# Third block of a three-block transformer kernel: output gate placed among the dense products, scratch moved out of the weight buffers, memory outcomes one direction behind, attention outputs divided instead of probabilities

## The reference, cut to what matters

```
h    = modulate(rms_norm(x), shift, scale)
proj = h @ w_in            # 1024 x 2832, columns: q 512, k 128, v 128, qk_m 1024, v_m 512, o_m 512, gates 16
y_attn = attention(rope(rms(q)), rope(rms(k)), v)          # 8 heads of 64, 2 key heads, not causal, softmax
qk     = silu(depthwise_conv5(qk_m))                       # queries and keys of the memory, 4 heads of 128
h_fw, h_bw = matrix-memory recurrence forwards and backwards, with input and forget gates, per head
y_mem  = rms(h_fw + h_bw) * norm_g * sigmoid(o_m)
x = x + g1 * (concat(y_attn, y_mem) @ w_out)
x = x + g2 * ((silu(h2 @ w_gate) * (h2 @ w_up)) @ w_down);  out = rms_norm(x)
```

## Time and profile before

| what | us |
|---|---|
| median of three runs (1934.21 to 1938.34) | 1935.97 |
| the profiled execution: its time | 1942.17 |
| its span, first to last instruction | 1940.4 |
| PE busy in the span | 1869.4 (96%) |
| DVE busy | 1168.7 (60%) |
| ACT busy | 737.5 (38%) |
| POOL busy | 127.6 (7%) |

### The profile page before, as it was taken

One profiled execution on the slowest core, in us unless ns is written; L12 is line 12 of the kernel. 1 busy time (PEld: TensorE's weight loads), 2 busy tenths in 40 slices (PEclk: granted clock), 3 DMA queues, 4 the chain that ended last, 5 costly groups with the idle time before them and its releaser, 6 DMA issues.

```text
span 1940.4 us, 22966 instructions
## 1 busy us (share of the span) xinstructions
PE 1869.4 (96%) x9180; PEld 1506.2 (78%) x9180; DVE 1168.7 (60%) x2110; ACT 737.5 (38%) x1154; POOL 127.6 (7%) x113
## 2 busy tenths in 40 slices
PE   9999999999999999999999999789898899999997
PEld 7775888878878788788888888677556698888885
DVE  4987686545566785578445446767775554333437
ACT  4458343322233434544222232535554352222221
POOL 0331000000000251000000000000230000000000
PEclk9999999999999999999999999899999899999998
DMA  6221425344441221224433432131001413323221
GB/s 204 66 71 34 158 90 193 131 144 138 152 153 45 87 66 44 87 87 152 130 108 118 139 113 89 27 106 44 1 1 66 141 33 102 105 87 109 87 87 44
DMA packets 118282, 186.17 MB, mean 96 GB/s; under 512 B 7472, under 2 KB 72176, under 8 KB 115104
## 3 DMA queue, kind: packets, MB, share of 16 engines
q1 hardware_dynamic: 116784, 179.90, 28.1%
q0 software_dynamic: 1392, 4.82, 0.8%
HBM read 182.57 MB, written 2.13 MB: 95 GB/s over the span
## 4 chain that ended last, share of the span: by engine, by line
PE 76%; DVE 16%; ACT 5%; issue 3%; POOL 0%; DMA 0%; DVEq 0%; ACTq 0%
PE bank L602 10%; PE bank L603 10%; PE bank L604 10%; PE bank L794 7%; PE bank L795 7%; PE bank L793 7%; DVE wl L1896 2%; PE bank L576 2%; PE bank L578 2%; PE bank L577 2%; PE bank L855 2%; PE bank L839 2%; DVE gb L2272 2%; DVE m L2270 1%; PE bank L827 1%
## 5 line engine op out<-in xcount | busy, mean ns | idle before, releaser
L1896 DVE TENSOR_TENSOR wl<-raw,wh 128x2048 fp32r<-128x2048 f32 (+1 forms) x137 | 307.6, 2251 | 195.2 <-ACT wh L1267 195.0
L1267 ACT ACTIVATE wh<-raw 128x2048 fp32r<-128x2048 f32 (+1 forms) x142 | 265.2, 1883 | 238.8 <-PE bank L795 90.5
L602 PE MATMUL bank<-xh,wh 128*128 128x512 f32 (+2 forms) x880 | 347.4, 395 | 2.2 <-DVE wl L1896 2.2
L603 PE MATMUL bank<-xh,wl 128*128 128x512 f32 (+2 forms) x880 | 346.7, 394 | 0.0
L604 PE MATMUL bank<-xl,wh 128*128 128x512 f32 (+2 forms) x880 | 346.7, 394 | 0.0
L795 PE MATMUL bank<-wh,ul 128*128 128x512 f32 x592 | 230.4, 389 | 0.0
L794 PE MATMUL bank<-wl,uh 128*128 128x512 f32 x592 | 230.4, 389 | 0.0
L793 PE MATMUL bank<-wh,uh 128*128 128x512 f32 x592 | 230.3, 389 | 0.0
L602 PEld LDWEIGHTS bank<-xh,wh 128*128 128x128 f32 (+2 forms) x880 | 164.9, 187 | 42.8 <-DVE wl L1896 3.1
L604 PEld LDWEIGHTS bank<-xl,wh 128*128 128x128 f32 (+2 forms) x880 | 165.0, 188 | 38.7
L603 PEld LDWEIGHTS bank<-xh,wl 128*128 128x128 f32 (+2 forms) x880 | 165.0, 187 | 38.1
(11 more groups left out here) (367 smaller groups left out, 3082.2 us busy)
## 6 DMA issues: line engine op xcount, KB each, us to landing
raw<-in_mlp_w_up SPq DMA_DIRECT2D x32, 1024.0 KB, 5.7
raw<-in_mlp_w_down SPq DMA_DIRECT2D x32, 1024.0 KB, 5.1
raw<-in_w_ada SPq DMA_DIRECT2D x24, 1024.0 KB, 5.2
raw<-in_b_w_in SPq DMA_DIRECT2D x12, 1024.0 KB, 5.2
raw<-in_w_in SPq DMA_DIRECT2D x11, 1024.0 KB, 5.1
raw<-in_w_gate SPq DMA_DIRECT2D x11, 1024.0 KB, 5.3
raw<-in_w_up SPq DMA_DIRECT2D x11, 1024.0 KB, 5.3
raw<-in_w_down SPq DMA_DIRECT2D x10, 1024.0 KB, 5.0
```

What stands on the lines that cost most here:

```text
L602: pe.matmul(o, H[:, k, c], xh[:, k, :], start=k == 0, stop=False)
L603: pe.matmul(o, L[:, k, c], xh[:, k, :], start=False, stop=False)
L1267: act.activation(slots[slot_of[i]][0][:, 0:n], raw[:, i % NRAW, 0:n], ACT.Copy).then_inc(*s_high.up(i))
L1896: dve.tensor_tensor(L[:, 0:n], raw[:, i % NRAW, 0:n], H[:, 0:n].bitcast(F), ALU.subtract).then_inc(*s_low.up(i))
```

## The change: what it does

Dense products: the 16 gate columns are appended to the keys' piece (two pieces of 4 x 272 columns instead of one of 8 x 256, `gates` and `ggT` go). The output gate's product `og` becomes an ordinary dense product between the second and third `conv`, its sigmoid is taken as its tiles are read. The order is `k2`, two `conv`, `og`, two `conv`, `v2`. All small jobs are numbered by step, from 0 to 31, and end with `v2`; the first two steps of `heads` are made at steps 28 and 30.

Middle: only `heads` and `memory` remain, in `side_by_side`: one step each for eight rounds, then one of `heads` and two of `memory`. The scratch moves to the halves of x (`xf`, which lies under `xh` and `xl`), to `pl` and to the halves of u (`rz`); `STm` and `Dd` get two buffers, `Db` three. The banks are shared out: 0 to 3 for scores, turned probabilities and inverses, 4 for the attention's output, 5 for `M`, 6 and 7 for `S` and `hm`. The outcomes of pair m are made during the scores of pair m + 1. `D` is one DVE instruction for four cells, and POOL masks it (`affine_select`). The probabilities are no longer divided: the inverses of the sums are turned, sent through DRAM to all partitions (`spread`), and POOL multiplies the outputs.

Tail: pieces of `w_out` are fetched and split during the middle. `first_column(0)` comes before `G` and `ymT`, `first_column(1)` behind them.

```diff
@@ weight_plan
-    plan_tok(w2, 512, 256)
-    slots(1, 0)
-    plan(w2, 0, 8, 2816, 16)
-    plan_tok(w2, 1792, 512)
-    for n in range(4):
+    for r0 in (0, 512):
+        plan(w2, r0, 4, 512, 256)
+        parts, nk, n = chunks[-1]
+        gates = w2[r0:r0 + 512, 2816:2832].rearrange("(k p) n -> p k n", p=P)
+        chunks[-1] = (parts + [(gates, n, 16)], nk, n + 16)
+    slots(0, 1)
+    for n in range(2):
         plan(w2, 0, 8, 768 + n * 256, 256)
     plan_tok(w2, 2304, 512)
...
+    plan_tok(w2, 1792, 512)
@@ buffers and banks
+def side_by_side(heads, mem, over):
+
+    live, n = [heads, mem], 0
+    while live:
+        for job in (heads, mem) if n < 8 else (heads, mem, mem):
+            if job in live and next(job, over) is over:
+                live.remove(job)
+        n += 1
...
+        B_UNITS, B_OUT, B_MAX, B_MEM, ANY = range(4), (4,), (5,), (6, 7), range(8)
...
+        DIVIDED = {"A": 7, "B": 4}
...
-        STm = rawf[:, 2048:4096].rearrange("p (b s) -> p b s", b=T)
+        PTs = [xf[:, 2048 * i:2048 * i + 2048].rearrange("p (b s) -> p b s", b=T) for i in range(2)]
+        STm = [xf[:, 4096 + 2048 * i:6144 + 2048 * i].rearrange("p (b s) -> p b s", b=T) for i in range(2)]
+        PB2 = [pl[:, 4 + i] for i in range(4)]
@@ tensor_program
+            def small_jobs():
+                for step in range(32):
+                    if step == 10:
+                        turn("qT2", tm, 4, s_step.at("rope q"))
+                    if step in (13, 14):
+                        gates(step - 13)
+                    if step == 20:
+                        turn("kT2", kd2, 2, s_step.at("rope k"))
+                    if step in (22, 26):
+                        gate_columns((step - 22) // 4)
+                    if step in (28, 30):
+                        next(heads)
+                    yield
...
                 start(0)
+                for m in range(len(MEM) + 1):
+                    for t in range(T):
                         yield
+                        if m < len(MEM):
+                            score(m, t)
+                        if m and t % 2 == 0:
+                            outcome(m - 1, t // 2)
+                        if m + 1 < len(MEM) and t == 2:
+                            start(m + 1)
+
+            side_by_side(heads, memory(), jobs)
...
+            first_column(0, cur.take(skip))
             for n, gc in enumerate((GC1, GC2)):
...
+            first_column(1, cur.take(skip, 2))
             cross("o3", UH, UL, 4, u_ready, 4, False, "x5", [("gate", 0, 0), ("upg", 0, 0)], xo, lambda t: s_act.at(("xo", t)))
@@ scalar_program
+                        if k < len(CELLS) and CELLS[k] in OFF:
+                            decay(*CELLS[k])
+                        if m + 1 < len(MEM) and t == T - 1:
+                            own(m + 1)
+                        if 0 < m <= len(MEM) and t % 2 == 0:
+                            size(m - 1, t // 2)
@@ vector_program, memory
+                        if m + 1 < len(MEM) and t == 3:
+                            own(m + 1)
+                        if m < len(MEM):
+                            weigh(m, t)
+                        if m and t % 2:
+                            divide(m - 1, t // 2)
+                        if m == 3 and t == 0:
+                            cur.reach(low, 2)
@@ POOL
-            attend("B", PB2, 8, False)
+                    w.wait_ge(*s_step.at(("D", m)))
+                    pool.affine_select(Dd[m % 2], Dd[m % 2], [[0, T], [1 - 2 * d, P]], ALU.is_ge, -BIG, 0, 2 * d - 1).then_inc(*s_pool.up(("D", m)))
@@ SP
-            w.wait_ge(*s_mm.at("middle"))
-            for i in range(core2, len(chunks)):
-                w.wait_ge(*low_of(i - NRAW))
-                fetch(i)
+                if i == mixed[2] + 3:
+                    for j in range(4):
+                        spread("B", j)
```

More of the change, by code:

```diff
@@ L114, in restart, with take @@
         self.order, self.user, self.before = list(range(8)), [None] * 8, {}
-    def take(self, name, hold=False):
-        b = self.order.pop(0)
+    def take(self, name, hold=False, among=range(8)):
+        b = next(b for b in self.order if b in among)
+        self.order.remove(b)
         if not hold:
@@ L1108, in small_jobs @@
-                yield from idle(2)
-                turn("kT2", kd2, 2, s_step.at("rope k"))
-                turned.append("k")
-                b = banks.take("ggT")
-                w.wait_ge(*banks.free("ggT", s_act.sem))
-                w.wait_ge(*s_act.at(("gates", 0)))
-                for t in range(T):
-                    step = pe.transpose(bank[b][:, t * 16:(t + 1) * 16], ggf[:, t * P:(t + 1) * P], ident[0:16, 0:16])
-                step.then_inc(*s_turn.up("ggT"))
-                yield from idle(3)
@@ L1118, in small_jobs @@
-                yield from gates(0)
-                yield from gates(1)
-            jobs.append(small_jobs())
-            gemm_tok("k2", 256, "x4", 1)
-            gemm_T("gates", "x4", 2)
-            gemm_tok("v2", 512, "x4", 2)
-            Wo = []
-            for n in range(4):
-                gemm_T(("conv", n), "x4", 2,
-                       (lambda: Wo.extend([cur.take(skip), cur.take(skip, 0)])) if n == 3 else None)
-            while len(turned) < 2:
-                tick(jobs)
@@ L1162, in start, with score @@
                     pe.matmul(bank[b][:, :], sel, Mr[d], start=True, stop=True).then_inc(*s_mm.up(("M", m)))
+                def score(m, t):
+                    hh = MEM[m][0]
+                    c0, c1_ = keys(m, t)
+                    b = banks.take(("S", m, t), False, B_MEM)
+                    w.wait_ge(*banks.free(("S", m, t), s_act.sem))
+                    w.wait_ge(*s_act.at(("conv", 7)))
+                    pe.matmul(bank[b][:, 0:c1_ - c0], mqk[:, 4 + hh, t * P:(t + 1) * P], mqk[:, hh, c0:c1_],
+                              start=True, stop=True).then_inc(*s_mm.up(("S", m, t)))
@@ new lines, in outcome @@
+                def outcome(m, tt):
+                    hh, d = MEM[m]
+                    b = banks.take(("hm", m, tt), False, B_MEM)
+                    w.wait_ge(*banks.free(("hm", m, tt), s_act.sem))
+                    w.wait_ge(*s_step.at(("ST", m, T - 1)))
+                    w.wait_ge(*s_act.at(("v2", T - 1)))
+                    w.wait_ge(*s_step.at("vx1"))
+                    for t in (2 * tt, 2 * tt + 1):
+                        src = list(range(0, t + 1) if d == 0 else range(t, T))
+                        o = (t % 2) * 256
+                        for q in src:
+                            step = pe.matmul(bank[b][:, o:o + 130], STm[m % 2][:, q, t * P:(t + 1) * P], vx[:, q, hh, :],
+                                             start=q == src[0], stop=q == src[-1])
+                    step.then_inc(*s_mm.up(("hm", m, tt)))
@@ L2600, in memory, with own @@
+            gemm_tok("k2", None, 1)
+            for n in range(2):
+                gemm_T(("conv", n), lambda j: evict_c(n, j), 1)
+            gemm_tok("og", None, 1)
+            for n in range(2, 4):
+                gemm_T(("conv", n), lambda j: evict_c(n, j), 1)
+            gemm_tok("v2", None, 1)
+            drain(jobs)
             def memory():
-                for job in rest:
-                    yield from job
-                def start(m):
+                def own(m):
                     hh, d = MEM[m]
-                    mk = CBT if d == 0 else CB
+                    M = bank[banks.of["M", m]][:, :].rearrange("p (t q) -> p t q", t=T)
@@ L2672, in vector_program @@
+            side_by_side(heads, memory(), jobs)
+            cur.take(low)
             w.wait_ge(*s_act.at(("hsq", T - 1, 3)))
```

789 lines of the change are left out of this document (355 added, 434 removed).

## The result

The changed kernel takes 1954.95 us (median of 4 runs, 1952.07 to 1958.85) where the kernel before takes 1936.11 on the same chip: a ratio of 1.0098, interval 1.0077 to 1.0119. It is 1% slower; 1912 us and "faster" were forecast. The profiled execution took 1955.38 us, its span 1953.6.

What follows compares the result with a forecast made beforehand. PE's list was taken as the bound, lengthened by waits of several engines. 111.8 + 116.2 + 5.8 = 233.8 against 257.5 us, 23.7 less: 1936.0 - 23.7 = 1912 us; own range 1902 to 1922, 8 in 10 for 1896 to 1928.

Steps and rivals of the forecast that it cites:

- dense products, less the earlier start: Dense products: 106.8 us of work, less 2.0 for the earlier start, plus 4 of waits and 3 of lower clock: 111.8.
- middle: Attention and memory stage: 94.6 us of PE work, 18.6 of holes and 3 for the clock behind them: 116.2.
- tail: Up to the first `w_out` product: `G` 3.7, turns 1.8, entry 0.3, both old waits gone: 5.8 us.
- the holes are hidden in 16 of 22 rounds: Middle: attention work in front of each two cells covers the bank waits; only rounds 16 to 21 bare, 11 us.
- A clock below 0.9 in the middle: Middle: listed among the observations that would show the prediction wrong; no time was attached to this sign.
- the clock falls: Rival, middle: lower clock in most later rounds, some 30 us lost, 1945 to 1960 us in all; chance 7%.
- the clock's term: Middle: 3 us for PE running at a lower clock behind the 18.6 us of holes.
- The 3.6 us that I put for `M`: Middle: next pair's `M` waits until ACT has read a backward pair's last `Db`, twice 1.8 us: 3.6.
- under PE's work: Middle: DVE's split of the `w_out` piece is hidden by PE's work; no time was put for it.
- a sum of differences is not touched by that: Baseline: the profiled execution's 6.2 us above the median 1936.0 was taken not to affect the predicted 23.7 us gain.
- The waits for the gates: Dense products: second direction's gates asked for some 3 us too early; 4 us put for this and the first `conv` piece.
- The mask: Middle: POOL's mask of `D` put at 1.8 us, between 0.7 and 3.7, making the next pair's hole 3 us.

Runs made afterwards that it cites:

- the kernel with the other phase: Changed kernel with one more single step at the start (n < 9 for n < 8), so late rounds hold cells 0, 1 or 2, 3: 1927.96 us.
- the run with `og` ahead: Kernel before, with only the output gate's product moved out of the middle, as a dense stretch ahead of it: 1949.42 us, ratio 1.0068.
- the fastest kernel: Changed kernel with division before weighing, memory pairs in rounds 1 to 14, gate columns and gates' turns later, `w_out` split behind `ym`: 1896.73 us.
- a kernel that differs by an earlier edit only: Changed kernel with division before weighing, memory pairs in rounds 1 to 14, second gate columns a step later: 1909.09 us; without the last edit 1918.51.

## Why the prediction was wrong

The stages, reckoned as there, from the first product of the keys to the first with `w_out`. The changed kernel starts this stretch 5.1 us earlier (1254.05 for 1259.19). The prediction put 2.0 for that.

| term | predicted | measured |
|---|---|---|
| dense products, less the earlier start | 111.8 | 119.6 - 5.1 = 114.5 |
| middle | 116.2 | 147.9 |
| tail | 5.8 | 5.9 |
| sum | 233.8 | 268.3 |

**The step that failed** is "the holes are hidden in 16 of 22 rounds". I had worked out the waits themselves correctly: S2 waits for the division of O0, S0 of the next pair for that of O1, 1.7 to 3 us each. But I took a late round to hold cells (0, 1) or (2, 3), so that an attention step stood in front of each cell that waits. It holds (1, 2) and (3, 0), since the generator's first `next` makes no cell. The order that is printed ahead of the prediction shows it: the cells come two by two without a row of the attention between them, and it is the second that needs the bank. So the mechanism was right and its place was wrong. In place of 18.6 us of waits there were 33.5, and the kernel with the other phase has 18.7.

**The clock** was the second part. A clock below 0.9 in the middle stood among the signs of being wrong, and it came. I put 3 us for it. With 94.6 + 3 = 97.6 us of busy time expected and 114.5 measured, it took nearly 17 more. My rival "the clock falls" named 1945 to 1960 us, "when the middle takes 140 us"; it took 148, and this rival comes nearest to what happened. I gave it 7%. Its number was better than its way there: it put some 30 us for the clock, of which 17 to 20 came, and most of the rest was waits that stood in the wrong rounds. I argued against it from the clock of the old middle; but there `og` filled the turns, and the run with `og` ahead (0.93 for 0.96, in one execution each) suggests that this filler was part of the reason. The Trainium skill (TensorE: Matmul & The Clock Gate, A second HAM failure mode: psum-queue depth-cycling) says that frequent short idle times between groups of matmuls, from cycling through PSUM banks, make the clock go back and forth; the trace agrees, with waits of 1.5 to 3.8 us for two banks and a clock of 0.85.

**Even in the right phase the forecast was too low.** The kernel that I had in mind exists: it is the one with the phase alone, 1928.0, the end of my range. Its middle takes 118.5 us from the first `M`, and 120.6 from the end of the dense products (1373.21 to 1493.82), 4.4 above 116.2. That is the clock's term, put at 3: PE is busy for 101.9 us in place of 97.6, at a clock of 0.93. The waits sum to 18.7 as against 18.6, but in part by luck. The 3.6 us that I put for `M` did not come. In their place stands one of 4.12 us, behind DVE's split of the piece of `w_out` (2.29 us), which I had put "under PE's work", at nothing. In the changed kernel this split stands before DVE's scaling of the scores, ahead of the wait of 2.21 us at L884.

The dense products of the changed kernel are 2.7 above: the waits are 7.9 (3.72, 2.47, 1.73) for 4, the busy time 111.7 for 109.8, the start 5.1 earlier for 2.0. But of the 5.1 only 1.8 are the shorter wait for the keys' piece. The other 3.3 are there already in the queries' product, which the edit does not touch:

```profile
1250.91 0.50 PE L1075 MATMUL bank<-wh,xh 128*128 128x512 f32 x1 [0.86 <-DVE xl L1949]
```

```profile
1247.59 0.50 PE L1094 MATMUL bank<-wh,xh 128*128 128x512 f32 x1 [0.86 <-DVE xl L1954]
```

The first row is of before, the second of the changed kernel, at the same place. So part of what looks like a gain is the slow execution of before.

The rest is the baseline. The profiled execution of before took 1942.2, 6.2 above the median of the shown runs, and I wrote that a sum of differences is not touched by that. It is: the runs of before with times of 1934 us have mean clocks of 0.988 and 0.989, those of 1940 and more 0.983 to 0.986, and I took clock losses of this very execution out as if every one had them. The profiled times differ by 1955.38 - 1942.17 = 13.2, the medians by 18.8; the 5.6 between is this, and the 3.3 above are the part of it that I can point at. The sum of the stages accounts for 268.3 - 257.5 = 10.8 of the 13.2; 2.4 us lie outside this stretch and were not followed.

**What was right.** The tail: `first_column(0)`, `G`, turns at full clock, both waits of the earlier trace rows gone, 0.40 left. The turns of queries and keys do not wait. The keys' piece: its wait fell from 2.54 to 0.73. The waits for the gates: I put 4 us in the dense products, and the wait at L1115 was 3.72; the second one, 2.47 at L1105, I did not see: DVE splits a piece first (2.29 us) where the gates' logarithm is due. The 1.73 us for another split I did not see either. The inverses' way through DRAM is hidden: no idle time of POOL's products is put down to it (below).

**The mask** was a size only (times on POOL are rough). I took 1.8 us between bounds of 0.7 and 3.7; in the changed kernel the groups of POOL in the middle show

```profile
L2850 POOL TENSOR_TENSOR pl<-pl,A 128x512 f32<-128x512 f32 x4 | 5.1, 1269 | 3.6 <-ACT pl L1375 3.6
L2858 POOL TENSOR_SCALAR_AFFINE_SELECT rz<-rz 128x512 f32<-128x512 f32 x8 | 5.1, 634 | 252.5 <-DVE rz L2587 252.5
```

634 ns, below its lower bound, DVE's 0.7. The Trainium skill (GPSIMD Engine Reference, Engine selection) had it right for this operation: one input, about line rate; with two inputs 1269, twice as long. Only the scaling by a column in the earlier trace rows, one input too, is out of that rule with 1834.

## What to carry to other kernels

When two generators are woven together by hand, count what the first `next` does, and read from the printed order which instruction stands between the one that holds a bank and the one that wants it: here one digit was worth 27 us. A dense product in a stage of small steps can also be a filler; whoever moves it out should reckon with the clock beside the waits. Here 33.5 us of waits came with some 17 us of lower clock, while the fastest kernel has 5.6 us of waits in its middle and a clock of 0.97. Move a long copy or split to a stage where its engine idles, not to a place one step further in the same round.

## What the runs showed of the hardware

The length of a wait alone did not tell its cost in clock. The same 3.73 us wait in the same list of instructions stood with 13.6 us at the lower level in one execution and with 3.4 us in another, of a kernel that differs by an earlier edit only; one execution of each was profiled. In the changed kernel, where a wait of 1.5 to 3.8 us came in nearly every late round, the clock was 0.50 for a stretch of ten us in which PE was 85% busy:

```profile
1440.00:1450.00 10.00, 7.79 (x32) 3.92 (x31) 4.42 (x7) 6.13 (x14) 0.00 (x0) 0.67 0.00 0
1450.00:1460.00 10.00, 8.51 (x23) 4.78 (x22) 1.96 (x8) 0.17 (x1) 0.00 (x0) 0.50 0.07 26
1460.00:1470.00 10.00, 7.33 (x27) 4.94 (x26) 5.65 (x15) 3.68 (x8) 0.63 (x1) 0.67 0.00 0
```

And useless products in front of a wait can pay: 12 pairs of them made the kernel 8 us faster. What decides whether the clock falls behind a given wait stays open here.
